# Attention output products over high and low halves joined to 512 columns; reciprocals and output written one unit later

## What is computed

```python
def dense_attention(q, k, v, sink):
    s = jnp.einsum('bqhgd,bkhd->bhgqk', qg, k).astype(jnp.float32) * (dh ** -0.5)
    p = jax.nn.softmax(s, axis=-1)
    o = jnp.einsum('bhgqk,bkhd->bqhgd', p.astype(v.dtype), v)
```

## Time and profile before

| | us |
|---|---|
| median of 3 runs | 4622.8 (4618.36 to 4623.26) |
| the profiled execution's own time | 4621.78 |
| its span | 4620.0 |
| mean granted TensorE clock, share of full | 0.961 |
| PE busy | 4249.3 (92%) |
| DVE busy | 2177.3 (47%) |
| ACT busy | 1573.8 (34%) |
| POOL busy | 900.7 (19%) |

### The profile page before, as it was taken

The page is one execution under the profiler, slowest core; times in us unless marked ns, Lnnn a source line. Parts: engine busy times, 40 slices in busy tenths (PEclk is TensorE's granted clock), DMA queues, the critical chain, the costliest instruction groups (busy, mean ns, idle before and its releaser), DMA issues.

```text
span 4620.0 us, 46359 instructions
## 1 busy us (share of the span) xinstructions
PE 4249.3 (92%) x18566; PEld 3097.0 (67%) x18566; DVE 2177.3 (47%) x3670; ACT 1573.8 (34%) x3044; POOL 900.7 (19%) x695
## 2 busy tenths in 40 slices
PE   7886889988999999988889999899989898999997
PEld 3446754757788888645457866565665677888886
DVE  2368844123556663336262327572655744333334
ACT  3566741132211111332332215353545633222222
POOL 2112225211434441016161000011000021000002
PEclk9998899999999999898979999999999999999999
DMA  5112242111334431311111210111000031111111
GB/s 196 51 58 92 82 150 87 28 64 64 105 105 116 117 114 48 109 56 46 55 46 55 78 45 22 34 63 54 14 23 19 19 128 32 51 46 55 46 39 62
DMA packets 257799, 308.89 MB, mean 67 GB/s; under 512 B 19072, under 2 KB 209936, under 8 KB 256304
## 3 DMA queue, kind: packets, MB, share of 16 engines
q1 hardware_dynamic: 238096, 227.15, 15.8%
q0 software_dynamic: 17408, 75.64, 5.2%
q10 hardware_dynamic: 2080, 3.15, 0.2%
HBM read 271.61 MB, written 34.28 MB: 66 GB/s over the span
## 4 chain that ended last, share of the span: by engine, by line
PE 63%; DVE 9%; ACT 5%; POOL 2%; issue 1%; DMA 0%; POOLq 0%; DVEq 0%; ACTq 0%
PE bank L194 61%; PE bank L197 2%; DVE Mx L214 1%; ACT at21P L203 1%; ACT at20P L203 1%; ACT Mx L203 1%; POOL sq L214 1%; DVE at21sm L232 1%; DVE at20sm L232 1%; DVE x L220 1%; DVE wfl L214 0%; DVE at20Pl L214 0%; DVE at21Pl L214 0%; DVE at11sm L232 0%; DVE at10sm L232 0%
## 5 line engine op out<-in xcount | busy, mean ns | idle before, releaser
L194 PE MATMUL bank<-h,wslot 128*128 128x512 f32 (+2 forms) x1616 | 682.9, 560 | 13.9 <-ACT h L203 3.8
L194 PE MATMUL bank<-hT,wslot 128*128 128x512 f32 (+3 forms) x1136 | 461.0, 562 | 13.9 <-DMA hT<-hspill 6.6
L194 PEld LDWEIGHTS bank<-h,wslot 128*128 128x128 f32 (+1 forms) x1616 | 288.1, 189 | 241.7 <-issue 225.6
L194 PEld LDWEIGHTS bank<-hT,wslot 128*128 128x128 f32 (+1 forms) x1136 | 211.7, 189 | 238.8 <-issue 232.3
L194 PE MATMUL bank<-ffn1h,wfh 128*128 128x512 f32 x704 | 279.8, 397 | 11.8 <-DVE ffn1l L220 10.9
L194 PE MATMUL bank<-ffn2h,wgh 128*128 128x512 f32 x704 | 276.3, 392 | 9.9 <-DVE ffn2l L220 9.5
L220 DVE SCALAR_TENSOR_TENSOR x<-bank,mod,x 128x512 f32<-128x512 f32 x224 | 164.3, 746 | 245.9 <-PE bank L194 245.4
L194 PE MATMUL bank<-ffn1l,wfh 128*128 128x512 f32 x704 | 274.9, 391 | 0.0
L194 PE MATMUL bank<-ffn2l,wgh 128*128 128x512 f32 x704 | 274.7, 390 | 0.0
L194 PE MATMUL bank<-ffn2h,wgl 128*128 128x512 f32 x704 | 274.6, 390 | 0.0
L194 PE MATMUL bank<-ffn1h,wfl 128*128 128x512 f32 x704 | 274.5, 390 | 0.0
(11 more groups left out here) (565 smaller groups left out, 9297.9 us busy)
## 6 DMA issues: line engine op xcount, KB each, us to landing
wslot<-in_w_in SPq DMA_DIRECT2D x40, 1024.0 KB, 5.5
ffn1t<-in_w_mod POOLq DMA_DIRECT2D x64, 512.0 KB, 4.8
wslot<-in_w_ffn_in SPq DMA_DIRECT2D x44, 512.0 KB, 5.2
Mx<-acsT SPq DMA_DIRECT2D x32, 512.0 KB, 4.8
at1w<-in_ada_w POOLq DMA_DIRECT2D x24, 512.0 KB, 4.7
wslot<-in_ffn_w_gate SPq DMA_DIRECT2D x22, 512.0 KB, 3.9
wslot<-in_ffn_w_up SPq DMA_DIRECT2D x22, 512.0 KB, 5.2
wslot<-in_w_ffn_out SPq DMA_DIRECT2D x20, 512.0 KB, 5.3
```

The source lines that it names most:

```text
L194: return Counted() if counting[0] else self.q.matmul(o, l, r, start=start, stop=stop)
```

## The change

1. The two rings `PTh`, `PTl` become one ring `PT` of four tiles with 1024 columns; a tile's high and low parts lie side by side (256 high, 256 low). ACT and DVE write them with an access pattern of 2 x 256.
2. `av` makes one product of 512 columns for each tile where it made two of 256. High-part products add up in columns 0 to 255 of the bank, low-part products in 256 to 511. It waits for both parts first.
3. `fin` on ACT makes a second copy: rows 0 to 63, columns 256 to 511, to `ot`. POOL adds the two copies (a new part, 16 additions a group). Low values by low weights (rows 64 to 127, columns 256 to 511) are left out of the sum; before, they were in it.
4. The spread of the reciprocals (`recip`) is no longer ahead of the unit's products. It writes the same columns 256 to 511 of the bank once ACT has read them, and stands in PE's list at step j = 1 of the next unit.
5. DVE's addition and its two multiplications (`out_y`), and with them the freeing of the bank, move from the end of the unit to step j = 2 of the next unit, ahead of that step's `turn`.

```diff
@@ AttGroup.__init__
-            self.PTh = Ring([sb(f"{nm}Ph{i}", [512], f32r) for i in range(4)])
-            self.PTl = Ring([sb(f"{nm}Pl{i}", [512], f32r) for i in range(4)])
+            self.PT = Ring([sb(f"{nm}Pt{i}", [1024], f32r) for i in range(4)])
...
+        def half(self, u, i, h):
+            na = min(2, len(self.segments(u[0])[1]) - i)
+            return self.PT[u, i][:, :].rearrange("p (a h n) -> p a h n", h=2, n=256)[:, 0:na, h, :]
...
@@ AttGroup.pe, av
                     for ev in self.bo.freed(u):
                         e.wait_ge(*ev)
-                    for x in range(2):
-                        e.wait_ge(*st.dve.after("rs", n, x0 + x))
-                        e.matmul(self.bo[u,][0:64, 256 + x * 128:384 + x * 128], self.sm[n, x0 + x][:, 8:9].to_broadcast([128, 64]), ident).then_inc(st.pe("r", u, x), 1)
-                        self.sm.give((n, x0 + x), st.pe.now())
...
                 e.wait_ge(*st.act.after("ph", u, i))
-                for a, c in enumerate(cs):
-                    e.matmul(b[:, 0:256], vhl[:, c * 128:(c + 1) * 128], ph[:, a * 256:(a + 1) * 256], start=i + a == 0, stop=False)
                 e.wait_ge(*st.dve.after("pl", u, i))
-                for a, c in enumerate(cs):
-                    t = e.matmul(b[:, 0:256], vhl[:, c * 128:(c + 1) * 128], pl[:, a * 256:(a + 1) * 256], start=False, stop=i + a == len(tiles) - 1)
+                for a, c in enumerate(tiles[i:i + 2]):
+                    t = e.matmul(self.bo[u,][:, :], vhl[:, c * 128:(c + 1) * 128], pt[:, a * 512:(a + 1) * 512], start=i + a == 0, stop=i + a == len(tiles) - 1)
...
+            def recip(u):
+                n, x0 = u
+                e.wait_ge(*st.act.after("o", u, 1))
+                for x in range(2):
+                    e.wait_ge(*st.dve.after("rs", n, x0 + x))
+                    e.matmul(self.bo[u,][0:64, hs[2 + x]], self.sm[n, x0 + x][:, 8:9].to_broadcast([128, 64]), ident).then_inc(st.pe("r", u, x), 1)
+                    self.sm.give((n, x0 + x), st.pe.now())
+            def late(i, j):
+                self.gate_pe(e, i, j)
+                if i and j == 1:
+                    recip(self.units[i - 1])
...
@@ AttGroup.dve
             def fin(u):
+                return
+            def out_y(u):
...
-                e.wait_ge(*st.act.after("o", u))
+                e.wait_ge(*st.pool.after("o", u))
+                e.wait_ge(*st.pe.after("r", u, 1))
                 e.tensor_tensor(o_[0:64, 256:512], self.bo[u,][0:64, 0:256], o_[0:64, 0:256], OP.add).then_inc(d("o", u), 1)
...
+            def late(i, j):
+                if i and j == 2:
+                    out_y(self.units[i - 1])
...
@@ AttGroup.act, fin
-                e.activation(o_[0:64, 0:256], self.bo[u,][64:128, 0:256], AF.Copy).then_inc(a("o", u), 1)
+                e.activation(o_[0:64, 0:256], self.bo[u,][64:128, 0:256], AF.Copy).then_inc(a("o", u, 0), 1)
+                e.activation(o_[0:64, 256:512], self.bo[u,][0:64, 256:512], AF.Copy).then_inc(a("o", u, 1), 1)
...
+        def pool(self, e):
...
+            for u in self.units:
+                o_ = self.ot[u,]
+                e.wait_ge(*st.act.after("o", u, 1))
+                e.tensor_tensor(o_[0:64, 0:256], o_[0:64, 0:256], o_[0:64, 256:512], OP.add).then_inc(st.pool("o", u), 1)
```

More of the change, by code:

```diff
@@ L3762, in av @@
                         e.wait_ge(*ev)
[L3763 to L3769 removed]
+                vhl, pt = self.at.vhl[self.g], self.PT[u, i]
                 e.wait_ge(*st.act.after("ph", u, i))
[L3771 to L3772 removed]
                 e.wait_ge(*st.dve.after("pl", u, i))
[L3774 to L3775 removed]
+                for a, c in enumerate(tiles[i:i + 2]):
+                    t = e.matmul(self.bo[u,][:, :], vhl[:, c * 128:(c + 1) * 128], pt[:, a * 512:(a + 1) * 512], start=i + a == 0, stop=i + a == len(tiles) - 1)
                 t.then_inc(st.pe("av", u, i), 1)
[L3777 to L3780 removed]
+                self.PT.give((u, i), st.pe.now())
+            def recip(u):
[9 more added lines that the diff above has]
+                    recip(self.units[i - 1])
+            self.walk(scores, lambda n, x: None, turn, av, lambda u: None, late)
+            recip(self.units[-1])
         def dve(self, e):
@@ L3813, in turn @@
             def turn(u, i):
[L3814 to L3817, removed]
                 e.wait_ge(*st.act.after("ph", u, i))
-                e.tensor_tensor(pl[:, 0:wd], self.bt[u, i][:, 0:wd], self.PTh[u, i][:, 0:wd].bitcast(f32), OP.subtract).then_inc(d("pl", u, i), 1)
+                e.tensor_tensor(self.half(u, i, 1), self.turned(u, i), self.half(u, i, 0).bitcast(f32), OP.subtract).then_inc(d("pl", u, i), 1)
                 self.bt.give((u, i), d.now())
             def fin(u):
+                return
+            def out_y(u):
                 n, x0 = u
-                o_ = self.ot[u,]
-                e.wait_ge(*st.act.after("o", u))
+                o_, m = self.ot[u,], self.g * 2 + x0 // 2
+                e.wait_ge(*st.pool.after("o", u))
+                e.wait_ge(*st.pe.after("r", u, 1))
                 e.tensor_tensor(o_[0:64, 256:512], self.bo[u,][0:64, 0:256], o_[0:64, 0:256], OP.add).then_inc(d("o", u), 1)
                 e.wait_ge(*d.now())
-                m = self.g * 2 + x0 // 2
                 for x in range(2):
-                    e.tensor_tensor(self.at.y[x * 64:x * 64 + 64, m * NL + n * 128:m * NL + (n + 1) * 128], o_[0:64, 256 + x * 128:384 + x * 128],
-                                    self.bo[u,][0:64, 256 + x * 128:384 + x * 128], OP.mult).then_inc(d("y", u, x), 1)
+                    e.tensor_tensor(self.at.y[x * 64:x * 64 + 64, m * NL + n * 128:m * NL + (n + 1) * 128], o_[0:64, hs[2 + x]],
+                                    self.bo[u,][0:64, hs[2 + x]], OP.mult).then_inc(d("y", u, x), 1)
                 self.bo.give((u,), d.now())
                 self.ot.give((u,), d.now())
-            self.walk(scores, soft, turn, lambda u, i: None, fin, lambda i, j: None)
+            def late(i, j):
+                if i and j == 2:
+                    out_y(self.units[i - 1])
+            self.walk(scores, soft, turn, lambda u, i: None, fin, late)
+            out_y(self.units[-1])
         def act(self, e):
@@ L3852, in turn @@
             def turn(u, i):
-                wd = min(2, len(self.segments(u[0])[1]) - i) * 256
-                ph = self.PTh.take(u, i)
-                for ev in self.PTh.freed(u, i):
+                self.PT.take(u, i)
+                for ev in self.PT.freed(u, i):
                     e.wait_ge(*ev)
                 e.wait_ge(*st.pe.after("t", u, i))
-                e.activation(ph[:, 0:wd], self.bt[u, i][:, 0:wd], AF.Copy).then_inc(a("ph", u, i), 1)
+                e.activation(self.half(u, i, 0), self.turned(u, i), AF.Copy).then_inc(a("ph", u, i), 1)
             def fin(u):
```

5 lines of the change are left out of this document (added).

## The result

| | us |
|---|---|
| before, median of 4 runs | 4623.0 (4618.4 to 4623.9) |
| changed, median of 4 runs | 4768.0 (4764.7 to 4773.8) |
| changed / before | 1.0316, 95% interval 1.0303 to 1.0329 |
| span of the changed kernel's profiled execution | 4762.9, before 4620.0 |
| mean granted TensorE clock | 0.950, before 0.961 |

The change costs 145 us. The forecast was 115, with the upper end of the range at +162.

The account below looks back on a forecast made before the run. PE nearly sets the pace, and the late-freed output bank closes a loop over PE, ACT and DVE. Window groups +59, dense +32, products -1 and clock +25 make +115: 4738 us on the median, range 4685 to 4785.

Parts of the forecast that it names:

- A: Start of a unit's first output product on PE; intervals before were 8.51 and 7.74 us in at10, 11.21 and 12.69 in at20.
- Dense groups: at20 and at21: intervals of 13.51 for 12.69 us and 12.8 for 11.21; 15.8 us each, +32.
- Window groups: at10 and at11: intervals of 11.02 for 8.51 us and 9.71 for 7.74; 29.5 us each, +59.
- 14 of a group's 15 intervals are of this kind: Window groups: 14 intervals between units lengthen by +2.25 us on average, +31.5 a group.
- The ends: After a group's last unit: output behind two copies, +0.4, and POOL's addition, 0.5; in the window groups' -2, dense ends -0.4.
- The clock: PE's stalls ahead of the first output product lower its granted clock; +25 us, bounds nothing and 68.
- The products: PE's 944 output products of 256 columns become 472 of 512, same columns streamed; -1 us.
- The cheap wide product: Rival: a wide product hides its fill behind the weight load, saving 57 us on the output products; 4680 us, chance 0.06.
- The dear pattern: Rival: 2 x 256 patterns cost 0.1 to 0.2 us an instruction, +19 to +38, up to 4775 us; chance 0.08.
- Clock untouched: Rival: the same loop over one bank with PE's clock unchanged, +90, 4713 us; chance 0.18.
- Faster: Rival: output bank free before PE asks for it, half of PE's 50 us idle time saved, 4597 us; chance 0.04.
- no change: Rival: the loop's excess is taken up by waits that vanish, time within 0.2% (9 us); chance 0.04.

Follow-up runs that it names:

- Experiment 1: Kernel before, with only DVE's output work and the freeing of the output bank moved to step 2 of the next unit; 4792.7 us, 1.0366.
- 3: Changed kernel, with DVE's output work one step earlier, at step 1 of the next unit; 4680.3 us, 1.0121.
- 5: Changed kernel with two output banks, taken from the score banks (dense groups) and the transpose banks (window groups); 4650.8 us, 1.0059.
- experiment 2: Changed kernel, with the third turn's transposes written ten times in the window groups to keep PE at work; 4736.2 us, 1.0243.
- experiment 9: Changed kernel with two output banks, without ACT's second copy and POOL's addition; 4652.9 us, 1.0065.
- experiment 7: Kernel before, in halves, with DVE's output work at step 2 of the next unit and two output banks everywhere; 4635.4 us, 1.0026.
- experiment 12: Experiment 7 with the reciprocals' two products moved to step 1 of the next unit, ahead of that step's turn; 4643.6 us, 1.0043.

## Why the prediction was right, and which terms were off

**The mechanism** was as written: one bank, freed from step 2 of the next unit, and PE at A waits for `y` in 14 intervals of a window group and 15 of a dense one. Experiment 1 shows that this piece alone makes the loss, 3 and 5 that an earlier output or a second bank takes most of it away.

**Dense groups, forecast +32.** The two intervals came as 13.49 and 12.64 against 13.51 and 12.8, and the groups as +16.7 and +15.4 = +32.1. The sum of rows held.

**Window groups, forecast +59.** By experiment 2 the loop without the low clock costs 35.4 and 34.3, so 70. The excess has two parts. The ten inner intervals are 0.21 and 0.31 us longer than worked out, mostly between first low part and output: 2855.95 - 2850.91 = 5.04 where I took 4.85 from the earlier trace rows. The intervals near a group's ends were not of the kind that I counted them as. The last three first products of at10, before and after:

```profile
2882.66 0.50 PE L194 MATMUL bank<-at10Ph,vhl 128*128 128x256 f32 x2
...
2887.69 0.50 PE L194 MATMUL bank<-at10Ph,vhl 128*128 128x256 f32 x2
...
2895.12 0.80 PE L194 MATMUL bank<-at10Ph,vhl 128*128 128x256 f32 x2
```

```profile
2928.60 0.73 PE L194 MATMUL bank<-at10Pt,vhl 128*128 128x512 f32 x2 [2.30 <-DVE y L214]
...
2938.48 1.20 PE L194 MATMUL bank<-at10Pt,vhl 128*128 128x512 f32 x4 [3.45 <-DVE y L214]
...
2944.14 2.07 PE L194 MATMUL bank<-at10Pt,vhl 128*128 128x512 f32 x4 [2.36 <-DVE y L214]
```

The last interval but one goes from 5.03 to 9.88 us (9.36 in experiment 2), where "14 of a group's 15 intervals are of this kind" gave it +2.25; the first two add 3.3 and 3.0. The last interval, forecast 2.4 shorter, went from 7.43 to 5.66, so 1.8 shorter, and in experiment 2 to 6.71.

**The ends.** 11.5 us more lie between the groups, and 1.7 behind the last. The end of at20 after the change:

```profile
3553.50 0.78 ACT L203 ACTIVATE rsx<-bank 64x256 f32<-64x256 f32 x2 [1.61 <-PE bank L194]
3554.34 0.65 PE L194 MATMUL bank<-cst,at20sm 128*64 128x128 f32 x4 [0.87 <-ACT rsx L203]
3554.36 0.71 POOL L214 TENSOR_TENSOR rsx<-rsx 64x256 f32<-64x256 f32 x1 [8.02 <-ACT rsx L203]
3555.11 0.41 DVE L214 TENSOR_TENSOR rsx<-bank,rsx 64x256 f32<-64x256 f32 x1 [2.49 <-POOL rsx L214]
```

DVE's addition starts 1.61 us behind the first copy, where it was 0.42 (3429.25 to 3429.67). The second copy is 0.4 of that, as forecast. The other 0.79 are POOL's addition and the reciprocals' products, side by side; the products had no price here. Without the copy and the addition, in experiment 9, it is still 1.19 us, the products alone taking 0.75 of them: the copy counted, the addition was hidden. In the window groups the end is longer by 1.9 us, from the start of the last product to the end of `y`, with the reciprocals at the low clock (1.12 us for 0.65). And the low clock lasts beyond the units: 0.81 in the 11.6 us behind at10 (2949.4 to 2961.0), where it was 1.00. From the end of the last `y` to the next group's first turn it takes 65.1 for 63.1 us behind at10 and 152.3 for 150.3 behind at11, 4 us that the clock term didn't hold.

**The clock, forecast +25 between 0 and 68.** The direction was right and the size short: 15.2 us in each window group, 30 in both, while the dense groups kept 0.96 and 0.97 and their forecast intervals, though PE stalls there 15 times for up to 2.7 us. My reserve for "not every stall is enough" was right for the dense groups; in the window groups nearly each interval had its slow stretch. So of the signs given, "granted clock in the four groups well below 0.98" came true in two of the four: the dense ones had stood at 0.97 before. Two numbers beside this term were loose. The stall was put at "about 2.6 to 2.9" from 11.02 and 9.71 less 7.5 to 8, which gives 1.7 to 3.5; it came as 2.5. And the range's ends are not quite what their descriptions add up to, 4690 and 4781 where 4685 and 4785 stand.

So 143 us of span against 115: +11 in the window loop, +5 in the window groups' clock, +13 between and behind the groups (4 of it clock), +1 for the products, and 2.6 less ahead of at10, whose first turn comes at 2768.9 instead of 2771.5. The misses did not cancel, as nearly all lay on the dear side; the total stayed in the range because each was small.

**The products, forecast -1.** A pair of wide products takes 3420.71 - 3420.16 = 0.55 us, the four narrow ones of experiment 7 3352.89 - 3352.34 = 0.55, as the columns of the earlier trace rows said. The cheap wide product, priced from rows at 4680, is not seen here; the Trainium skill (TensorE: Matmul & The Clock Gate, "Back-to-back issue gap") gives 131 ns for 512 columns in a stream with weight loads, and this trace doesn't agree, with 0.55 us for two.

**The other rivals.** The dear pattern fell: copies and subtractions over 2 x 256 take 0.60 and 0.69 us in the timeline above, as in the earlier trace rows. "Clock untouched" fell with 0.86. "Faster" and "no change" needed the bank to be free ahead of A; PE waits 36.2 us for it in at10.

**What was priced at nothing.** ACT's second copy and POOL's addition cost nothing that shows off the ends, once there is a second bank (experiment 9). The spread of the reciprocals, "moved and not doubled, in PE's time that is now slack", holds only while PE has slack: once the stall is gone the new place costs 5.7 us a dense group (experiment 12). In the stalled kernel it is probably a gain: experiment 1 against the change says so, but the two differ in more than that.

## What to carry to other kernels

When work that frees a buffer is moved later in an engine's list, close the loop on paper: from the buffer's first use through each engine to its release, with the rows' durations; if the sum is longer than the interval now, every interval gets that length, whatever the busy shares say. Add what the stalled TensorE loses in clock behind each stall, and test that term by keeping it busy with repeated work of no effect. A piece moved into another engine's wait is free only as long as that wait lasts, and a second buffer is worth what the ring it is taken from can spare.

## What the runs showed of the hardware

- More work made the kernel faster: 432 more transposes in the window groups took 32 us off, by the granted clock (0.86 to 0.97).
- Somewhat shorter stalls cost far less: 14 of mostly 2.5 us brought a window group from 0.99 to 0.86, while 15 of mostly 1.35 and 1.8 us left a dense group at 0.96, where it had 0.97. Where the dense group's stalls were mostly 2.1 and 2.3 us (experiment 1), it stood at 0.92. The work between the stalls differs too, so no bound follows from this.
- POOL's addition of 64 partitions by 256 elements takes 724 ns, that of 128 partitions 723: half the partitions save nothing.
